# The mLSTM maximum rows of a decoder trunk, spread by one fp32r product in place of a plain fp32 product

## The reference, cut to what matters

```python
b = jnp.cumsum(lft, axis=-1)                       # lft = log_sigmoid(forget gate)
dmat = jnp.where(causal, b[..., :, None] - b[..., None, :] + it[..., None, :], -jnp.inf)
mt = jnp.maximum(inter, jnp.max(dmat, axis=-1))    # running maximum m_t
w = jnp.exp(dmat - mt[..., None])
qk = jnp.einsum('bhtd,bhsd->bhts', qt, kt) * w
h = num / jnp.maximum(jnp.abs(den), jnp.exp(-mt))[..., None]
```

## Time and profile before

| | before |
|---|---|
| median of 3 runs (range) | 1113.03 us (1112.18 to 1113.85) |
| profiled execution, first to last instruction | 1108.9 us |
| PE busy | 1078.4 us, 97% |
| DVE busy | 870.7 us, 79% |
| ACT busy | 662.6 us, 60% |
| POOL busy | 114.7 us, 10% |
| DMA | 285.89 MB, 258 GB/s in the mean |

### The profile page before, as it was taken

How to read it: one execution, slowest core, us unless ns; L and a number is a source line. 1 busy time by engine, 2 the same in 40 slices (tenths; PEclk the granted TensorE clock), 3 DMA queues, 4 the chain that set the end, 5 groups by cost and what they waited for, 6 DMA issues and landing times.

```text
span 1108.9 us, 15258 instructions
## 1 busy us (share of the span) xinstructions
PE 1078.4 (97%) x5352; PEld 875.6 (79%) x5352; DVE 870.7 (79%) x1139; ACT 662.6 (60%) x848; POOL 114.7 (10%) x160
## 2 busy tenths in 40 slices
PE   7999999999999999999999999999999999999996
PEld 5777777678878888888886888878978888888883
DVE  5256765788799999999999453654699999999997
ACT  5224444523488888878876413222488888778872
POOL 2010000222120000011013000000120000010013
PEclk9999999999999999999999999999999999999998
DMA  9742222112389999999999522332189999999985
GB/s 326 196 149 77 86 86 77 62 72 77 115 304 392 406 396 397 408 393 410 399 386 327 177 79 77 114 100 90 77 305 392 406 396 396 409 395 410 400 338 211
DMA packets 78643, 285.89 MB, mean 258 GB/s; under 512 B 17687, under 2 KB 17687, under 8 KB 62204
## 3 DMA queue, kind: packets, MB, share of 16 engines
q1 hardware_dynamic: 66396, 241.64, 57.0%
q0 software_dynamic: 8464, 30.42, 8.3%
q10 hardware_dynamic: 3728, 13.11, 2.9%
HBM read 266.27 MB, written 20.20 MB: 258 GB/s over the span
## 4 chain that ended last, share of the span: by engine, by line
PE 67%; DMA 15%; DVE 10%; ACT 3%; issue 2%; POOL 2%; POOLq 0%; DVEq 0%; SPq 0%; ACTq 0%
PE ps L1836 20%; PE ps L1838 19%; PE ps L1837 19%; DMA ring<-in_exp_w_gate 10%; DVE w_split L1073 5%; ACT w_split L672 2%; DMA arena<-h_rows_dram,arena 2%; DMA arena<-y_rows_dram,arena 1%; PE ps L2171 1%; DMA y_rows_dram<-arena 1%; PE ps L2085 1%; POOL arena L634 1%; PE ps L2107 1%; PE ps L1811 1%; PE ps L1920 1%
## 5 line engine op out<-in xcount | busy, mean ns | idle before, releaser
L1073 DVE TENSOR_TENSOR w_split<-ring,w_split 128x1024 fp32r<-128x1024 f32 x428 | 505.1, 1218 | 46.8 <-ACT w_split L672 39.1
L672 ACT CAST w_split<-ring 128x1024 fp32r<-128x1024 f32 x428 | 441.8, 1052 | 128.6 <-PE ps L1838 90.2
L1836 PE MATMUL ps<-w_split,hT 128*128 128x512 f32 (+1 forms) x976 | 385.6, 395 | 3.7 <-DVE hT L1581 1.7
L1838 PE MATMUL ps<-w_split,hT 128*128 128x512 f32 (+1 forms) x976 | 377.7, 387 | 0.0
L1837 PE MATMUL ps<-w_split,hT 128*128 128x512 f32 (+1 forms) x976 | 376.8, 386 | 0.0
L1836 PEld LDWEIGHTS ps<-w_split,hT 128*128 128x128 f32 x976 | 183.5, 188 | 43.8 <-issue 2.9
L1838 PEld LDWEIGHTS ps<-w_split,hT 128*128 128x128 f32 x976 | 183.3, 188 | 38.0
L1837 PEld LDWEIGHTS ps<-w_split,hT 128*128 128x128 f32 x976 | 183.7, 188 | 34.1
L1836 PE MATMUL ps<-hT,w_split 128*128 128x512 f32 (+1 forms) x384 | 144.8, 377 | 1.8 <-DVE hT L1109 1.0
L1837 PE MATMUL ps<-hT,w_split 128*128 128x512 f32 (+1 forms) x384 | 142.8, 372 | 0.0
L1838 PE MATMUL ps<-hT,w_split 128*128 128x512 f32 (+1 forms) x384 | 142.8, 372 | 0.0
(11 more groups left out here) (271 smaller groups left out, 914.0 us busy)
## 6 DMA issues: line engine op xcount, KB each, us to landing
ring<-in_exp_w_gate SPq DMA_DIRECT2D x64, 1024.0 KB, 12.5
ring<-in_exp_w_up SPq DMA_DIRECT2D x64, 1024.0 KB, 12.5
ring<-in_exp_w_down SPq DMA_DIRECT2D x64, 1024.0 KB, 13.2
ring<-in_w_in_even SPq DMA_DIRECT2D x14, 1024.0 KB, 11.4
y_rows_dram<-arena ACTq DMA_DIRECT2D x32, 384.0 KB, 7.0
ring<-in_w_in_odd SPq DMA_DIRECT2D x12, 1024.0 KB, 8.7
ring<-in_w_out_even SPq DMA_DIRECT2D x4, 1024.0 KB, 4.7
h_rows_dram<-arena POOLq DMA_DIRECT2D x8, 512.0 KB, 3.2
```

The source lines that it names most:

```text
L672: ins = s.copy(hi_of(c), raw(c))
L1073: ins = v.tensor_tensor(lo_of(c), raw(c), hi_of(c).bitcast(F32), ALU.subtract)
L1836: mm(out, a[0], b[0], start=start, stop=False)
L1838: return mm(out, a[0], b[1], start=False, stop=stop)
```

## The change

The selector and the four rows move into `w_gates_split`, in fp32r. Each row -M is taken apart into three fp32r parts whose sum is the row, on partitions 0 to 3, 32 to 35 and 64 to 67. The selector `head_pick` is one column per head on 68 partitions, with ones where a part of that head's row stands, and is broadcast to 128 columns in the product. GpSimd no longer clears and fills `head_row`, so that both counts fall by one. The parts and the selector are made by nine VectorE instructions between `splits(at_last_job(2))` and `job(11)`; `link` lets the next instruction wait until this one is complete.

```diff
-        head_row = part(8192, HEADS, P)[0:HEADS]
         neg_m_row = part(8704, T)[0:HEADS, :]
+        gates_flat = w_gates_split[:, :, :, :].rearrange("p s k n -> p (s k n)")
+        neg_m_parts, head_pick = gates_flat[0:64 + HEADS, 0:T], gates_flat[0:64 + HEADS, T:T + HEADS]
...
-                    sp.wait_ge(zeros_ready, 4)
+                    sp.wait_ge(zeros_ready, 3)
...
-            g.memset(head_row[:, :, :], 0.0).then_inc(zeros_ready, 1)
...
-            pool.wait_ge(zeros_ready, 7)
+            pool.wait_ge(zeros_ready, 6)
...
-            g.affine_select(out=head_row[:, :, :], in_=head_row[:, :, :], compare_op=ALU.not_equal, fill=1.0, base=0,
-                            pattern=[[-1, HEADS], [0, P]], channel_multiplier=1).then_inc(consts_ready, 1)
...
             splits(at_last_job(2))
+            link(v.tensor_scalar(head_pick, ident[0:64 + HEADS, 0:HEADS], 0.0, None, ALU.mult))
+            for q in (0, 32, 64):
+                v.tensor_copy(head_pick[q:q + HEADS, :], ident[q:q + HEADS, q:q + HEADS])
+            link(v.tensor_copy(neg_m_parts[0:HEADS, :], neg_m_row[:, :]))
+            link(v.tensor_tensor(f, neg_m_row[:, :], neg_m_parts[0:HEADS, :].bitcast(F32), ALU.subtract))
+            link(v.tensor_copy(neg_m_parts[32:32 + HEADS, :], f))
+            link(v.tensor_copy(soft_part, neg_m_parts[32:32 + HEADS, :].bitcast(F32)))
+            link(v.tensor_tensor(neg_m_parts[64:64 + HEADS, :], f, soft_part, ALU.subtract))
             job(11)
             splits(at_start(3))
...
-            dve.wait_ge(consts_ready, 8)
+            dve.wait_ge(consts_ready, 7)
...
-            pe.wait_ge(consts_ready, 8)
+            pe.wait_ge(consts_ready, 7)
...
-                mm(ps[:, 3, :], head_row[:, h, :], neg_m_row[:, :], start=True, stop=True).then_inc(m_row_full, 1)
+                mm(ps[:, 3, :], head_pick[:, h:h + 1].broadcast_to([64 + HEADS, P]), neg_m_parts, start=True,
+                   stop=True).then_inc(m_row_full, 1)
```

## The result

The changed kernel takes 1117.76 us (median of 6 runs, 1115.03 to 1120.97), the kernel before 1112.61 us (1109.52 to 1114.47). The ratio is 1.0050, 95% interval 1.0033 to 1.0067: 5.6 us slower, with 3.7 to 7.5. The forecast was slower by 2.9 us. In a second set of 9 runs the ratio was 1.0056, so over both about 6 us. The direction and every duration of the sum came out; what was left out of the sum, TensorE's clock, costs nearly as much again.

A forecast was written before the change was run, and what follows sets the result against it. TensorE, busy 97% of the span, was taken as the bound, with VectorE's zero-slack chain ahead of `scores(0)`. VectorE's +3.5 us less 0.6 us of row-product gains gave +2.9 us, 1115.9 us, range 1113.9 to 1118.0.

The forecast's parts named there:

- VectorE's block: Nine VectorE instructions between the splits and `job(11)`: 3.50 us added, bounds 3.2 and 4.1.
- All of it reaches `scores(0)`: VectorE has zero slack before the gate columns' copy, so `scores(0)` starts 3.5 us later and the delay carries to the end.
- The row products: Four heads' products save 3.7 us of TensorE work, but only 0.6 us reaches the end, bounds 0.2 and 1.5.
- The 0.23 between like neighbours: Heads 2 and 3: one fp32r product of 512 columns takes a step of 0.23 us between like products.
- The cover: Heads 2 and 3: TensorE idles for VectorE's add instead of multiplying, leaving gains of 0.13 and 0.08 us.
- head 0's gain: Behind head 0's row product, the chain through ScalarE's square limits the gain to 0.4 us, bounds 0 and 0.82.
- The 0.9 us for loads that might not be hidden: Row products: selector loads cost nothing beside the product ahead; otherwise 0.23 us each, 0.9 in all.
- The clock: Behind the gate-columns wait, the sum counted no loss from TensorE's clock; a fall was left to rival A.
- rival A: Clock falls in the 3.9 us gap before `scores(0)`, costing about 1.5 us more: 1117.4 us; chance 0.25.
- The start: First dummies begin about 1.1 us sooner, idle before the first real product grows to 2.1 us; effect 0.
- Span and median: Whole kernel: the median of the runs lies 4.1 us over the profiled span, before and after the change.

The follow-up runs named there:

- e8: Kernel before with the row products of heads 2 and 3 cut from 512 columns to 16: ratio 0.9992, -0.9 us.
- e2: Changed kernel with 27 instead of 11 dummy products ahead of the wait for the gate columns: ratio to before 1.0038, +4.2 us.
- e1: The changed kernel timed again, nothing else changed: ratio to the kernel before 1.0056, +6.2 us.
- e7: Kernel before plus the nine VectorE instructions at their place, with old product and old start: ratio 1.0044, +4.9 us.
- e3: Kernel before without the 11 dummy products ahead of the wait for the gate columns: ratio 1.0005, +0.6 us.
- e11: Kernel of e6 plus 6 dummy products ahead of the wait for the first head's values: ratio to before 0.9992, -0.9 us.
- e12: Kernel of e11 once more, unchanged: ratio to the kernel before 0.9983, -1.9 us.
- e6: Changed kernel with the VectorE block behind the gate columns' copy and 14 instead of 11 dummies at the start: ratio to before 0.9985, -1.7 us.
- e10: Changed kernel with the nine VectorE instructions moved ahead of `splits(at_last_job(2))`: ratio to before 1.0022, +2.4 us.
- e5: Kernel before with GpSimd's two old-selector operations behind the other constants, so the first dummies begin 1.05 us sooner: ratio 1.0002, +0.2 us.
- e9: Changed kernel with 14 dummy products at the start and 27 ahead of the gate columns: ratio to before 1.0032, +3.6 us.

## Why the prediction was right or wrong

- **VectorE's block: right.** 3.50 us forecast, 3.49 in the trace. The three 4x4 copies took 0.51; a conversion of 4x512 took 0.42, as the TENSOR_SCALAR it was taken from, and not 0.68. The copies to other groups of partitions took 0.17 us each from start to start and did not overlap, as the rule of the Trainium skill quoted there (VectorE: DVE Perf Modes, Two Vector instructions with no wait between them) has it.
- **All of it reaches `scores(0)`: right.** The wait grew from 0.40 to 3.90 us, and nothing before 209 us gives any of it back.
- **The row products: right in total and in place.** 0.42, 0, 0.12 and 0.07 us against 0.4, 0, 0.13 and 0.08. An fp32r product is one record, with 0.32 to 0.41 us to the next start at heads 0 and 1. The 0.23 between like neighbours can't be read at heads 2 and 3, since TensorE waits behind both. The cover there is shown by e8 and by the waits of 0.62 and 0.69 us for L1281. That head 0's gain runs over ScalarE's square was not tested apart. The 0.9 us for loads that might not be hidden, "in the bounds" by the text, are not in the sum of the upper bound; nothing of them was seen.
- **The clock: the step that failed.** The sum let TensorE run on at the upper level behind a gap ten times as long as before and put that at nothing; the fall stood beside it as rival A, with a chance of 0.25 and a price of 1.5 us. At this place it fell in each profiled execution with a gap of 2.9 us or more and in none of those with 1.2 us or less. The table shows what it cost. In the mean of the executions e2 has it at 2.2 us (standard error 0.7), and a fall behind the gap is thus most of the 2.7 us that the sum missed. The price of 1.5 came from the start, read as 11 dummies at the low level; in fact the first eight start some 0.43 us apart and the last ones 0.22. It fits two of the four falls, and in the other two the low stretch was longer.

| profile | wait for the gate columns | behind at `scores(0)` | behind at head 0's row product | lost between |
|---|---|---|---|---|
| changed | 3.90 | 4.75 | 7.57 | 2.82 |
| e1 | 3.89 | 6.20 | 7.70 | 1.50 |
| e7 | 3.90 | 3.54 | 5.95 | 2.41 |
| e3 | 2.90 | 0.13 | 1.74 | 1.61 |
| the nine others (before is the measure) | 0.40 to 1.23 | -0.01 to 3.48 | -0.11 to 3.41 | -0.15 to 0.02 |

- **The clock elsewhere.** The length of a gap alone does not decide. Behind the 1.4 us wait for head 0's values, which all but e11 and e12 have, e3, e6 and e10 have a low stretch, and the nine others have none. The mean clock says what it costs in the whole: 0.9921 before and 0.9887 after. Since the low level is half the upper one, the time at it is twice the missing share, 17.5 and 25.2 us, and at most half of the 7.7 us between them, 3.8, is lost (an estimate). 6.2 in the means less 3.8 leaves 2.4 us for all else, beside the 2.9 of the sum.
- **The start: wrong in a part.** That the chain "does not move: 0" held only for the chain of waits. The early dummies lost 1.25 us to the clock in the profiled execution (e5 1.3), though the gap ahead of the first transposes only went from 1.04 to 1.39 us and not to the forecast 2.1, since the dummies themselves took 4.73 us instead of 4.12. In the timed runs this loss is not told from nothing.
- **Span and median.** The 4.1 us between them were partly chance, the profiled execution being a short one. Execution by execution the distance is 1.8 us before and 2.0 after. The kernel before alone spreads over 11 us (1107.58 to 1118.55), with its longer executions at the lower mean clock.

## What to carry to other kernels

Work that lengthens a wait of TensorE is to be priced twice: by the wait, and by the products behind it at half the pace; here the second was more than half of the first. Dummy products ahead of a wait have to be counted out anew whenever the wait, or their own start, moves. And a new block belongs where its engine is idle ahead of its reader's need, not where its input happens to be ready: the same nine instructions some 3 us later delayed nothing.

## What the runs showed of the hardware that was not expected

A start earlier by 1.05 us, with no more work, brought the clock down in five of six profiled executions with 11 dummies, and in none of four with 14 (e6, e9, e11, e12). Behind the gap 512-column products went on starting every 0.42 us for some us, with dense work in hand. And TensorE busy throughout did not keep the clock up at 790 us (0.69 with 10.00 of 10.00 us busy). The same kernel on the same chip, with nothing changed, spreads over 11 us, and its longer executions are those with the lower mean clock.
